# A two-layer decoder trunk without the matmuls on constants that nobody reads

## The reference

```python
for i in range(DEPTH):                       # DEPTH = 2, x is 1 x 256 x 1024, float32
    h = rms_norm(x, attn_norm[i])
    x = x + (swa_sink_attention(h, ...) if i == 0 else stick_breaking_attention(h, ...))
    h = rms_norm(x, ffn_norm[i])
    x = x + (swiglu(h, ...) if i == 0 else moe_swiglu(h, router, w_gate, w_up, w_down))
return rms_norm(x, final_norm)

def moe_swiglu(h, router, w_gate, w_up, w_down):
    logits = t @ router                      # 256 tokens x 8 experts
    top_vals, top_idx = lax.top_k(logits, 2)
    ...
    for e in range(8):                       # expert width 3584
        out = out + combine[:, e:e + 1] * swiglu(t, w_gate[e], w_up[e], w_down[e])
```

## Time and profile before

| | us |
|---|---|
| median of 3 runs | 1424.26 |
| lowest, highest | 1423.34, 1424.68 |
| the profiled execution, device time | 1424.04 |
| its span in the trace | 1422.2 |
| PE busy in it | 1387.0 (98%) |
| DVE, ACT busy | 1093.3, 923.4 |
| mean granted clock | 0.993 |

### The profile page before, as it was taken

One profiled execution on the slowest core, in us unless ns is written; L12 is line 12 of the kernel. 1 busy time (PEld: TensorE's weight loads), 2 busy tenths in 40 slices (PEclk: granted clock), 3 DMA queues, 4 the chain that ended last, 5 costly groups with the idle time before them and its releaser, 6 DMA issues.

```text
span 1422.2 us, 19285 instructions
## 1 busy us (share of the span) xinstructions
PE 1387.0 (98%) x7161; PEld 1163.0 (82%) x7161; DVE 1093.3 (77%) x823; ACT 923.4 (65%) x762; POOL 47.0 (3%) x37
## 2 busy tenths in 40 slices
PE   8989999999989999999999999999999999999997
PEld 5869999979876888888888888888888888888886
DVE  4856454464546888988888888898889888889886
ACT  4555433353554777777777777777777777777775
POOL 2110000000000000100000000000000001000000
PEclk9999999999999999999999999999999999999999
DMA  9334553655314999999999999999999999999993
GB/s 343 128 118 163 190 194 121 213 197 189 126 57 180 345 373 370 364 394 374 364 394 387 359 377 394 363 358 396 382 352 396 375 376 374 389 372 365 393 371 130
DMA packets 183378, 430.47 MB, mean 303 GB/s; under 512 B 7131, under 2 KB 10261, under 8 KB 183334
## 3 DMA queue, kind: packets, MB, share of 16 engines
q1 hardware_dynamic: 179280, 416.31, 80.2%
q0 software_dynamic: 3072, 11.06, 2.7%
q10 hardware_dynamic: 982, 2.49, 0.5%
HBM read 422.47 MB, written 7.36 MB: 302 GB/s over the span
## 4 chain that ended last, share of the span: by engine, by line
PE 89%; DVE 5%; issue 2%; DMA 2%; ACT 1%; POOL 0%; DVEq 0%; ACTq 0%
PE bank L1340 87%; DVE low L533 2%; PE bank L1706 2%; DMA kv_area<-bias_dram 1%; DVE h L973 1%; PE bank L1495 0%; PE bank L1675 0%; DMA qT<-in_onehot 0%; DMA bias_dram<-work 0%; ACT work L776 0%; POOL work L552 0%; DVE work L1261 0%; DVE peak L1059 0%; DVE inT_low L1002 0%; PE bank L1392 0%
## 5 line engine op out<-in xcount | busy, mean ns | idle before, releaser
L533 DVE TENSOR_TENSOR low<-raw,high 128x2048 fp32r<-128x2048 f32 (+1 forms) x397 | 899.7, 2278 | 230.4 <-ACT high L528 229.3
L528 ACT CAST high<-raw 128x2048 fp32r<-128x2048 f32 (+1 forms) x397 | 754.8, 1903 | 297.0 <-PE bank L1340 297.0
L1340 PE MATMUL bank<-high,inT_high 128*128 128x512 f32 x1000 | 395.2, 395 | 4.7 <-DVE low L533 2.6
L1340 PE MATMUL bank<-high,inT_low 128*128 128x512 f32 x1000 | 390.4, 390 | 0.0
L1340 PE MATMUL bank<-low,inT_high 128*128 128x512 f32 x1000 | 390.0, 390 | 0.0
L1340 PEld LDWEIGHTS bank<-high,inT_high 128*128 128x128 f32 x1000 | 188.2, 188 | 45.0 <-DVE low L533 4.3
L1340 PEld LDWEIGHTS bank<-high,inT_low 128*128 128x128 f32 x1000 | 188.1, 188 | 40.0
L1340 PEld LDWEIGHTS bank<-low,inT_high 128*128 128x128 f32 x1000 | 188.4, 188 | 37.8
L1340 PE MATMUL bank<-high,hid_high 128*128 128x512 f32 x528 | 207.2, 392 | 0.0
L1340 PE MATMUL bank<-high,hid_low 128*128 128x512 f32 x528 | 205.7, 390 | 0.0
L1340 PE MATMUL bank<-low,hid_high 128*128 128x512 f32 x528 | 205.5, 389 | 0.0
(11 more groups left out here) (177 smaller groups left out, 657.3 us busy)
## 6 DMA issues: line engine op xcount, KB each, us to landing
raw<-in_moe_w_gate SPq DMA_DIRECT2D x112, 1024.0 KB, 7.3
raw<-in_moe_w_up SPq DMA_DIRECT2D x112, 1024.0 KB, 7.4
raw<-in_moe_w_down SPq DMA_DIRECT2D x112, 1024.0 KB, 7.2
raw<-in_sb_w_qkv SPq DMA_DIRECT2D x12, 1024.0 KB, 5.4
raw<-in_ffn_w_down SPq DMA_DIRECT2D x11, 1024.0 KB, 4.9
raw<-in_ffn_w_gate SPq DMA_DIRECT2D x10, 1024.0 KB, 5.2
raw<-in_ffn_w_up SPq DMA_DIRECT2D x10, 1024.0 KB, 5.1
raw<-in_swa_w_qkv SPq DMA_DIRECT2D x4, 1024.0 KB, 14.2
```

The costliest lines, as they stand in the source:

```text
L528: nc.scalar.copy(high[n % SPLIT][:, :, 0:c], raw[r][:, :, 0:c]).then_inc(high_done, 1)
L533: nc.vector.tensor_tensor(low[n % SPLIT][:, :, 0:c], raw[n % RAW][:, :, 0:c], high[n % SPLIT][:, :, 0:c].bitcast(F32), ALU.subtract).then_ ...
L1340: return nc.tensor.matmul(out, lhsT, rhs, start=start, stop=stop, **kw)
```

## The change

All matmuls on constants whose results nobody reads are taken out, with the two functions that issue them. Nothing else is altered: no wait on another engine's work, no DMA, no bank of PSUM. The 1 + 3 at the begin, the 3 x (2 + 1) around the inner norms, the 3 during the picks and the 1 before the gather go: 17 matmuls, 34 instructions.

```diff
-            def warm_up(n):
-
-                b = begin(pe, ("hT0", 3))
-                for _ in range(n):
-                    mm(b, ones[:, :], ones[:, :].unsqueeze(1).to_broadcast([P, 4, P]), True, True)
-
             pe.wait_ge(ones_set, 1)
-            warm_up(1)
             pe.wait_ge(gain_loaded, 16)
...
             filled(mm(b[0:H, 0:2 * WINDOW], rel[:, :], onehot, True, True), "bias rows")
-            warm_up(3)
...
-            def keep_clock(key, n):
-
-
-                b = begin(pe, key)
-                for _ in range(n):
-                    mm(b, ident, consts[:, 0:HALF], True, True)
-
             def transposed_h(k):
-                if k > 0:
-                    keep_clock((f"hT{k}", 3), 2 if k else 3)
                 transposed(h, f"hT{k}", lambda n: pe.wait_ge(h_ready, TB * DH * k + n))
                 arriving.extend((f"hT{k}", j) for j in range(4))
-                if k > 0:
-                    keep_clock((None, ("fy", 0, 0), ("q1", 0), "logits by expert")[k], 1)
...
             filled(ins, "logits")
-            keep_clock("places", 3)
             pe.wait_ge(picks_ready, 1)
...
-            keep_clock(("first gather", 1), 1)
             pe.wait_ge(place_ready, 1)
             first_gather()
```

## The result

| | before | after |
|---|---|---|
| median (runs) | 1423.83 us (22) | 1426.03 us (22) |
| lowest to highest | 1422.66 to 1426.31 | 1423.87 to 1427.84 |
| profiled execution: device time, span | 1424.04, 1422.2 | 1426.42, 1424.6 |
| mean granted clock in it | 0.993 | 0.987 |

The ratio is 1.0014, with a 95% interval of 1.0008 to 1.0021: the change makes the kernel 2.2 us slower, between 1.1 and 3.0. That is within the 1425.7 to 1433.5 of the prediction and less than half of its 5.0 us.

What follows compares the result with a forecast made beforehand. PE bounds the kernel, busy 98% of the span; the removed matmuls fill holes, and emptied holes may drop its clock. 0 + 0.8 + 1.2 + 1.1 + 0.1 + 1.8 = 5.0 us, 1424.26 + 5.0 = 1429.3, range 1425.7 to 1433.5.

Steps and rivals of the forecast that it cites:

- Begin: Four matmuls at the begin: slow key and value matmuls end later, but the wait for `hankel` hides it; cost 0.
- rival B: Not slower: a shorter hole before `hankel` keeps the clock up, gaining 1.6 us; about 1423.5; chance 0.08.
- Norm 1: Three matmuls around norm 1: between 0 and one low stretch of 1.7 us beginning at 112.4; taken as 0.8.
- Norm 2: Three around norm 2: a 3.5 us hole brings a low stretch over transposes and layer 1's query matmuls; net +1.2 us.
- Norm 3 and the router: Three there: the router's 16 instructions may run at the low clock; half, in two cases of three, 1.1 us.
- Places and gather: Clock falls in the picks' hole: places +0.1 us, gather's 32 instructions 2.1 less 0.3 hidden, +1.8.
- The rule weighed: Trainium skill's rule: the full clock does not engage for transposes; by it every norm is empty between weight matmuls, giving rival C.
- Rival C: Each place falls and low stretches last 6.8 us: +11, 1435.3; chance 0.12.
- A: Only the picks' hole lowers the clock, the norms' transposes hold it: +2.4, 1426.7; chance 0.17.
- the forecast: Some places fall, +2.9 to +8 us; chance 0.63.
- the signs named ahead: 0.50 within 300 to 309 and about 447 to 454, gather over 5 us, no `token` wait, first expert 3 to 7 later.

Runs made afterwards that it cites:

- norm2_out: Kernel before without only the three constants matmuls around norm 2: 1425.44 us, ratio 1.0008.
- begin_out: Kernel before without only the four matmuls on ones at the begin: 1423.53 us, ratio 0.9998.
- norm1_out: Kernel before without only the three constants matmuls around norm 1: 1423.89 us, ratio 1.0000.
- norms_out: Kernel before without only the nine constants matmuls around the three inner norms: 1425.00 us, ratio 1.0006.
- fitted_no_norms: fill_fitted without the constants matmuls around the inner norms: 1420.21 us, ratio 0.9973 to the kernel before.
- fitted_none: fill_fitted without any constants matmuls that the change takes out, only those in the new holes staying: 1420.95 us, ratio 0.9982 to the kernel before.
- picks_out: Kernel before without only the three constants matmuls during the picks, the one before the first gather staying: 1424.01 us, ratio 0.9999.
- fill_fitted: Kernel before with constants matmuls added in further holes, counts fitted: one per stick-breaking hole, four ahead of norm 2's transposes, none behind: 1417.54 us, ratio 0.9958.
- routing_out: Kernel before without only the three constants matmuls during the picks and the one before the first gather: 1424.92 us, ratio 1.0008.

## Why the prediction was right in its mechanism and too high in its size

**Counted over all traces.** The kernel before, after, and the twelve others:

| place | constants there | fell in | lost in the trace when it fell |
|---|---|---|---|
| norm 1 | in | 0 of 9 | |
| norm 1 | out | 4 of 5 | 1.4 to 2.0 us |
| norm 2 | in, as before | 3 of 6 | 1.1 to 1.3 (0.75 of it ahead of the first query matmul) |
| norm 2 | four ahead, none behind | 0 of 3 | |
| norm 2 | out | 5 of 5 | 1.0 to 1.2, in norm2_out 1.9 |
| router | out | 0 of 4 | |
| picks and gather | all out | 4 of 4 | 1.2 to 2.1 |

The losses at norm 2 are taken from its first scaled piece to the first `mask_tri` matmul, 51.87 us where the clock is up.

**Begin, predicted 0.** Right: 0.9998 and, with the rest quiet, 1417.04 against 1417.54. The slow keys and values end before `hankel` lands. The gain of 1.6 us that rival B hoped for did not come: the clock fell at 26.1 in begin_out and was at 0.50 over the toeplitz matmuls as before.

**Norm 1, predicted 0.8 between 0 and 1.7.** No trace has the middle: it was 0 in one and 1.4 to 2.0 in four. The upper bound was too low, since it took a stretch of 3.4 us that begins at 112.4, behind the transposes; in the kernel after the stretch began at 108.4, before the second half of them, and was 6.8 us long. How often the place falls, one trace each of five different kernels cannot say; by the mean clock of its executions, norm1_out seems to have held in most of them.

**Norm 2, predicted 1.2.** In the kernel after it is 5.02 + 127.72 us against 4.78 + 126.76 with the clock up: 1.2. As predicted, but I took it against a kernel before whose clock is up there. That was so in the one execution I had. In three of the six traces with these constants in place it is not: the matmul behind the transposes then runs at the low clock itself and stands in the way, 5.53 us instead of 4.78, and 1.1 to 1.3 us are lost in all, as much as without the constants in four traces of five. This is one part of what the change gives back.

**Norm 3 and the router, predicted 1.1.** Wrong: this term of the sum measured 0. In all four kernels without constants at norm 3 (after, norms_out, fitted_no_norms, fitted_none) the router's 16 instructions kept their 3.6 us: no fall at this place. The holes are those of norm 1, so I cannot say from these runs why norm 1 falls and norm 3 does not.

**Places and gather, predicted 0.1 + 1.8.** The 2.1 of the kernel after is near the predicted 1.9 by luck, since errors cancel. The stretch from the first of the places to the gather lost 1.0, since the clock fell before them (0.1 was predicted for ten instructions that I called latency), and the gather 2.5 instead of 2.1; but the cover behind them was 1.4 and not 0.3, as picks_out showed.

**The sum.** With the clock otherwise up, the places of the kernel after come to 1.9 + 1.2 + 0 + 2.1 = 5.2 us, and I had predicted 5.0. That the two agree is luck: norm 1 was 1.1 too low and the router 1.1 too high. What was mis-sized is the step "on the profiled execution's 1424.04": it treats all other low stretches as fixed. They are not: the one after 80 us lasted 6.8 us in three of the eight kernels that left it alone and 3.4 in the other five (81.2 to 81.6 against 80.2 to 80.4 us from the toeplitz matmuls to norm 1), and the stick-breaking attention had none, one or two of them, in kernels that differ nowhere near. Between the two profiles 2.6 us came back by these (0.9 after 80 us, 1.6 in the stick-breaking attention, rounded) and 0.3 ahead of the toeplitz matmuls. With the rates and losses of the table as if they were means, norm 1 at four in five of 1.7, norm 2 at 1.3 less half of 1.2, and routing at 1.5 give 3.6 us, an estimate; measured are 2.2, between 1.1 and 3.0. That low stretches are a fixed number which only moves is excluded by fill_fitted, which has none between the first rise and the last matmul.

**Where the missing part may lie.** The places do not fall independently of each other. In the three traces where the stretch after 80 us is 6.8 us long (before, norm1_out, picks_out), norm 2 held with its constants in and the stick-breaking attention had one low stretch; norm1_out, the only kernel without constants at norm 1 in which norm 1 held, is one of the three. In begin_out and routing_out, where it is 3.4 us, norm 2 fell and the attention had two: from norm 2 to norm 3 they take 135.0 us instead of the 133.18 of before. The kernel after has the short stretch after 80 us too, and takes 132.74; norms_out, likewise, 133.48; norm2_out 135.11. So against traces of its own kind the kernel after gained 2.3 us between norms 2 and 3, and its loss is 1.9 - 2.3 + 2.1 = 1.7 us. That is near the measured 2.2 and rests on one or two traces of each kind; it is not shown to be the cause. The mean granted clock of every execution points the same way. It averages 0.9925 in 82 executions of the kernel before and 0.9872 in the 22 of the kernel after. Since 0.50 counts for half, this is 21.4 and 36.5 us at the low clock, 15.1 more, where the three new stretches of the profile alone are 23.9 us long. So on average they do not all come at full length, or others go when they come; the means do not say which.

**The rule weighed.** The transposes of norm 1 in norm1_out stood in a stretch of 5.5 us with no other work, at 1.00 to its end and beyond, and those of norm 3 did in all four kernels without constants there. At norm 2, behind 3.4 us of nothing, the clock was low and they did not bring it back before the query matmuls. By the rule of the Trainium skill (TensorE: Matmul & The Clock Gate, Part 4: PE-mode transpose), transposes do not count as busy time in the way other matmuls do. The trace agrees with it at norm 2, and not at norm 3. Rival C, built on every place falling, came true at three of four places, and was right that the low stretches there last 6.8 us and more; but they cost no more than 2.1 each, where C had 2.2 for norm 2 and 3.1 for places and gather.

**The other rivals.** A (only the picks lose, 1426.7) hit the time better than the forecast, and for a reason that the profile of the kernel after excludes: norms 1 and 2 both fell. A time that agrees shows no mechanism. B needed the clock to hold during the picks, where it fell in all four traces.

**The signs and the chances.** Of the signs named ahead, most came: 0.50 from 303.0 to 309.7 and from 446.4 to 456.5, a gather of 6.31 us, no wait for `token` in front of `slot_sums`, and the same distance from the first expert to the end (966.70 and 966.74 us). One did not: the first expert's matmul came 2.3 us later and not 3 to 7. And the prediction gave 0.77 to a loss above 2.85 us and 0.21 to one within it; measured was 2.2, inside the less likely part.

## What to carry to other kernels

Matmuls that nobody reads earn their place only where they fill a hole in front of work that PE sets the time of; here three of the groups were worth 1 to 2 us each when they held the clock, and the one at the begin nothing, since a DMA is waited for right behind it. Fit their number to the hole: with the clock down at norm 2, the one behind the transposes brought the first query matmul 0.5 us later than with none there (5.53 against 5.03 us), and two instead of one behind a wait for a bank held PE up by 0.9 us more at each of two places. Filling all holes, also those the kernel had left, gave 1417.54 us, 0.42% under the kernel before, and without the four at the begin 1417.04: the best versions of this study.

A single profile of a kernel whose clock comes and goes is a draw. Before a sum is made on it, ask of every low stretch in it whether it is there each time, and compare traces of the same kind; the mean granted clock of each execution tells how typical a profile is.

## What the runs showed of the hardware that I had not expected

The same instructions with the same waits fell to 1.2 GHz in one execution and not in another (norm 1 without constants, 4 of 5 traces). A hole of 1.8 us in the stick-breaking attention was followed by a fall in some executions (before, at 394.2) and by none at the same place in another (after, at 395.9). Every recorded low stretch between the first rise and the last matmul was 3.4, 6.8 or 10.2 us long. And ahead of the first recorded rise, at 11.3 to 19.3 us, the profile's clock column reads 1.00 while the matmuls take the times of 1.2 GHz.
